# Prompt attention in a hybrid decoder layer: values as weights on column halves, probabilities scaled one step ahead of their turn, output feature-major

## The reference, cut to what matters

```python
s = jnp.einsum('bnqkgd,bnskd->bnkgqs', qb, kband, preferred_element_type=jnp.float32) * (HEAD_DIM ** -0.5)
p = _sink_softmax(s, sinks, mask[None, :, None, None])      # exp(s - m) / (sum + exp(sink - m))
o = jnp.einsum('bnkgqs,bnskd->bnqkgd', p.astype(v.dtype), vband)
...
h = h + (ga * (oa @ w_oa) + gb * (ob @ w_ob)) @ w_out
```

## Time and profile before

| | |
|---|---|
| median of 3 runs | 3545.36 us (3543.18 to 3545.62) |
| the profiled execution, its own time | 3547.21 us |
| span of the profiled execution, first to last instruction | 3545.4 us |
| busy: PE, DVE, ACT, POOL | 97%, 49%, 35%, 7% of the span |
| granted PE clock, mean | 0.977 |
| granted PE clock in the delta stage: first group (210 to 555 us), second group (1216 to 1384 us) | 0.86, 1.00 |

### The profile page before, as it was taken

How to read it: one execution, slowest core, us unless ns; L and a number is a source line. 1 busy time by engine, 2 the same in 40 slices (tenths; PEclk the granted TensorE clock), 3 DMA queues, 4 the chain that set the end, 5 groups by cost and what they waited for, 6 DMA issues and landing times.

```text
span 3545.4 us, 52950 instructions
## 1 busy us (share of the span) xinstructions
PE 3430.2 (97%) x21860; PEld 2912.6 (82%) x21860; DVE 1730.3 (49%) x3115; ACT 1257.6 (35%) x2414; POOL 253.2 (7%) x289
## 2 busy tenths in 40 slices
PE   6979999999999999999999999999999999999998
PEld 6868779999999777888878877888887877788886
DVE  3844334543446744554345744554344755454343
ACT  3323324322223544432224544432223544432222
POOL 1211000000002101000001201000000311000000
PEclk9868989999999999999999999999999999999999
DMA  4101012322233211333233211233234211233232
GB/s 171 60 20 50 31 32 71 104 90 85 87 133 105 68 43 43 107 101 95 94 132 121 74 43 43 84 114 98 92 93 165 78 44 42 73 114 99 96 95 81
DMA packets 88558, 298.66 MB, mean 84 GB/s; under 512 B 12272, under 2 KB 14272, under 8 KB 87664
## 3 DMA queue, kind: packets, MB, share of 16 engines
q1 hardware_dynamic: 88320, 295.28, 25.8%
HBM read 283.63 MB, written 12.62 MB: 84 GB/s over the span
## 4 chain that ended last, share of the span: by engine, by line
PE 51%; issue 11%; ACT 2%; DMA 1%; DVE 1%; SPq 0%; POOLq 0%; POOL 0%; DVEq 0%
PE bank L734 42%; PE bank L922 1%; PE bank L1159 1%; DMA raw<-in_wstream 1%; PE bank L1150 1%; PE bank L1162 1%; PE bank L897 1%; PE bank L1093 1%; PE bank L909 1%; PE bank L1067 1%; PE bank L1073 0%; PE bank L950 0%; ACT junk L1510 0%; PE bank L995 0%; PE bank L1104 0%
## 5 line engine op out<-in xcount | busy, mean ns | idle before, releaser
L734 PE MATMUL bank<-hnT,wh 128*128 128x512 f32 (+1 forms) x3520 | 931.4, 352 | 0.0
L1675 DVE TENSOR_TENSOR wl<-raw,wh 128x1024 fp32r<-128x1024 f32 x480 | 595.0, 1240 | 662.5 <-ACT wh L1316 661.1
L734 PE MATMUL bank<-xnT,wh 128*128 128x512 f32 (+2 forms) x2560 | 742.1, 376 | 13.9 <-DVE d_dT L1927 11.1
L734 PEld LDWEIGHTS bank<-hnT,wh 128*128 128x128 f32 x3520 | 619.4, 188 | 91.4 <-issue 0.2
L1316 ACT CAST wh<-raw 128x1024 fp32r<-128x1024 f32 x480 | 500.4, 1043 | 392.7 <-PE bank L734 337.8
L734 PE MATMUL bank<-hnT,wl 128*128 128x512 f32 (+1 forms) x1760 | 622.2, 354 | 0.0
L734 PEld LDWEIGHTS bank<-xnT,wh 128*128 128x128 f32 x2560 | 450.7, 194 | 86.7 <-DVE d_dT L1927 12.4
L734 PE MATMUL bank<-hid,wh 128*128 128x512 f32 (+1 forms) x1760 | 468.2, 354 | 5.2 <-DVE wl L1675 4.0
L734 PE MATMUL bank<-xnT,wl 128*128 128x512 f32 (+2 forms) x1280 | 469.3, 367 | 0.0
L734 PEld LDWEIGHTS bank<-hnT,wl 128*128 128x128 f32 x1760 | 330.6, 188 | 45.8
L734 PEld LDWEIGHTS bank<-hid,wh 128*128 128x128 f32 x1760 | 309.5, 188 | 53.2 <-DVE wl L1675 6.0
(11 more groups left out here) (309 smaller groups left out, 3916.5 us busy)
## 6 DMA issues: line engine op xcount, KB each, us to landing
raw<-in_wstream SPq DMA_DIRECT2D x472, 512.0 KB, 3.5
xr<-in_x_prompt SPq DMA_DIRECT2D x16, 512.0 KB, 5.6
xT<-in_xT SPq DMA_DIRECT2D x4, 2048.0 KB, 12.2
hT<-in_xT SPq DMA_DIRECT2D x4, 2048.0 KB, 8.6
out_yp_out<-hT SPq DMA_DIRECT2D x16, 512.0 KB, 2.9
raw<-in_wstream SPq DMA_DIRECT2D x8, 528.0 KB, 3.8
Sb<-in_state_delta SPq DMA_DIRECT2D x1, 2048.0 KB, 10.3
out_ds_out<-Sb SPq DMA_DIRECT2D x1, 2048.0 KB, 6.4
```

Source lines behind the costliest of these rows:

```text
L734: ins = nc.tensor.matmul(*a, **k)
L1675: v_.tensor_tensor(wl[n % HL][:, 0:m], raw[:, n % RAW, 0:m], wh[n % HL][:, 0:m].bitcast(F32), ALU.subtract).then_inc(sem("lo_done"), 1)
```

## The change

It has four parts.

1. The value products swap their operands. `vn` (128 keys by 64 features) is the weight, put on the left or the right half of the array's columns, and `pTm` moves, two heads (256 columns) at a time. Four products instead of eight; the result in bank 4 is feature-major, the two key/value heads in the two partition halves.
2. The denominators can't be applied behind such a product, so DVE scales the probabilities in `sc` (128x1024) between exp and transposes, in a step of its own, `scale`; the copy of bank 4 becomes a plain one.
3. To make room for that step the tables are moved: in `IN_DELTA` transposes from 6 and 11 to 7 and 12, the first values from 7 to 8; in `IN_CONV` transposes from 6 and 8 to 7 and 9, values from 7 and 9 to 8 and 10; in `IN_DELTA_S` inputs, scores and exps one step earlier.
4. The 16 transposes of the `z` stage go in each group; ACT and DVE read `qkv` in place of a bank.

```diff
-IN_DELTA = dict(inputs=2, scores=(3, 8), exp=(5, 10), transposes=(6, 11), values=(7, 13))
-IN_DELTA_S = dict(inputs=1, scores=(2, 6), exp=(3, 7), transposes=(4, 8), values=(5, 13))
+IN_DELTA = dict(inputs=2, scores=(3, 8), exp=(5, 10), scale=(6, 11), transposes=(7, 12), values=(8, 13))
+IN_DELTA_S = dict(inputs=0, scores=(1, 5), exp=(2, 6), scale=(3, 7), transposes=(4, 8), values=(5, 13))
-IN_CONV = dict(inputs=4, scores=(5, 7), exp=(5, 7), transposes=(6, 8), values=(7, 9))
+IN_CONV = dict(inputs=4, scores=(5, 7), exp=(5, 7), scale=(6, 8), transposes=(7, 9), values=(8, 10))
...
             def att_transposes(t, gk):
                 r = round_of(t, gk)
-                pe.wait_ge(*made("pexp_done", r + 1))
+                pe.wait_ge(*made("att_p", 2 * t + gk + 1))
...
                 claim(4, "oa_done", r + 1)
-                for y in range(GQ):
-                    ps = slice(HD * (y % NKV), HD * (y % NKV + 1))
-                    for s in range(2):
-                        last = nc.tensor.matmul(bank[4][:, HD * y:HD * (y + 1)], pTm[:, 2 * y + s, :], vn[:, s, ps],
+                turned = pTm[:].rearrange("p (x y) n -> p x y n", x=2)
+                for s in range(2):
+                    for half in range(NKV):
+                        ps = slice(HD * half, HD * (half + 1))
+                        last = nc.tensor.matmul(bank[4][ps, 0:2 * P], vn[:, s, ps], turned[:, :, 2 * half + s, :],
                                                 start=s == 0, stop=s == 1)
...
                 feature_block("z", j, (1, 0)[j % 2], 2, "z_ps", "z_silu", j + 1)
-                b = (6, 7)[j % 2]
-                claim(b, "oT_lo", (j + 1) * (1 + F))
-                for t in range(NT):
-                    last = nc.tensor.transpose(bank[b][:, P * t:P * (t + 1)], qkv[:, t + 1, P * j:P * (j + 1)], c("ident"))
-                last.then_inc(sem("oaT_ps"), 1)
...
-                act.wait_ge(*made("oaT_ps", j + 1))
-                act.copy(oT[0][:, j, MAIN], bank[(6, 7)[j % 2]][:]).then_inc(sem("oT_hi"), 1)
+                if j == 0:
+                    act.wait_ge(*made("oa_done", round_of(NT - 1, NKV - 1) + 1))
+                act.copy(oT[0][:, j, MAIN].rearrange("p (t n) -> p t n", t=NT), qkv[:, 1:, P * j:P * (j + 1)]).then_inc(sem("oT_hi"), 1)
...
                     r = round_of(t, gk)
+                    if k == where["scale"][gk]:
+                        denominators(r, GQ)
+                        settle()
+                        v_.tensor_tensor(sc[:], sc[:], bc(st[:, 20:20 + GQ], [P, GQ, 2 * P]), ALU.mult).then_inc(sem("att_p"), 1)
                     if k == where["transposes"][gk]:
-                        denominators(r, GQ)
                         dve.wait_ge(*made("pT_ps", r + 1))
...
                         dve.wait_ge(*made("pv_ps", r + 1))
-                        v_.tensor_tensor(qkv[:, t + 1, 256 * gk:256 * (gk + 1)].rearrange("p (a e) -> p a e", a=GQ),
-                                         bank[4][:, 0:GQ * HD].rearrange("p (a e) -> p a e", a=GQ),
-                                         bc(st[:, 20:20 + GQ], [P, GQ, HD]), ALU.mult).then_inc(sem("oa_done"), 1)
+                        v_.tensor_copy(qkv[:, t + 1, 2 * P * gk:2 * P * (gk + 1)], bank[4][:, 0:2 * P]).then_inc(sem("oa_done"), 1)
...
-                v_.tensor_tensor(oT[1][:, j, MAIN], bank[(6, 7)[j % 2]][:], oT[0][:, j, MAIN].bitcast(F32), ALU.subtract).then_inc(sem("oT_lo"), 1)
+                v_.tensor_tensor(oT[1][:, j, MAIN].rearrange("p (t n) -> p t n", t=NT), qkv[:, 1:, P * j:P * (j + 1)],
+                                 oT[0][:, j, MAIN].bitcast(F32).rearrange("p (t n) -> p t n", t=NT), ALU.subtract).then_inc(sem("oT_lo"), 1)
```

More of the change, by code:

```diff
@@ L101 @@
         (0, 4, 4):
-            "oaT_ps ob_hi ob_lo prod_done z_silu",
+            "ob_hi ob_lo prod_done z_silu",
         (0, 5, 4):
@@ L110 @@
         (0, 8, 8):
-            "hn_hi hn_lo hsq_done mix_f mix_hi mix_lo pT_rd0 sqc_done sum_ps ysq_done",
+            "att_p hn_hi hn_lo hsq_done mix_f mix_hi mix_lo pT_rd0 sqc_done sum_ps ysq_done",
         (0, 9, 0):
@@ L395, in program @@
         A_done QK_done X_done Y_ps Y_done m_done PT_ps PT_done X_ps X_rd DT_ps XY_done WU_ps WT_rd U_rd WS_ps u_done ob_rd
-        QB_zero small_p o_ps dS_ps S_done osq_done orr_done ob_done gate_ps gate_e gate_done z_ps z_silu obT_ps ob_lo oaT_ps
+        QB_zero small_p att_p o_ps dS_ps S_done osq_done orr_done ob_done gate_ps gate_e gate_done z_ps z_silu obT_ps ob_lo
         oT_hi oT_lo prod_done mix_ps mixS_ps mix_rd mix_f mix_hi mix_lo state_out act_g dve_g gate_eS act_pre
```

## The result

The changed kernel takes 3576.43 us (median of 4 runs, 3574.91 to 3577.99), the kernel before beside it 3545.49 us (4 runs, 3543.18 to 3546.72): ratio 1.0089, interval 1.0077 to 1.0101. It is 31 us slower, where +12.5 us was forecast and the range ended at 3572. The profiled execution's span is 3575.2 us against 3545.4, so the two traces differ by 29.8 us.

A forecast was written before the change was run, and what follows sets the result against it. PE, busy 97% of the span, was taken to bound the kernel by its work plus waits. Terms -5.2 + 6 - 1 + 1 + 8.7 + 3 = +12.5 us on 3547.2 gave about 3557.5 us as median, range 3545 to 3572.

The forecast's parts named there:

- Value products: PE's value step in each of 32 rounds: 1.82 us falls to 1.17, gaining 0.65 a round if PE isn't waiting.
- z blocks: Removed transposes save PE 0.43 us in each of blocks 0 to 2, nothing in block 3; 5.2 us over four groups.
- Scaling on DVE: DVE's added step takes about 1.2 us; probabilities are ready 1.6 us after DVE turns to them.
- Delta tiles: Nine tiles of groups 2 to 4: new PE waits outweigh cheaper values, +0.65 us a tile, +6 us, bounds -1 to +13.
- Rival B: Waits are covered because DVE reaches the sum earlier against PE; delta tiles -8 us, total about 3541 us; chance 0.08.
- Beside tile S: Cheaper values against attention inputs now ahead of the Gram product and added scaling: +1 us, between -3 and +3.
- Conv stages: Groups 2 to 4: second round's scores wait 3.3 us for just-filled banks; +2.9 us a stage, +8.7, between +6 and +11.
- the end of the stage keeps its distances, so nothing is given back: Conv stages: after the second round's transposes find their probabilities ready, the stage's end keeps its distances; nothing is given back.
- The clock: More PE waits and holes may bring clock dips, one earlier dip being worth 1.9 us: +3 us, 0 to +10.
- rival A: Column halves don't overlap, so a value step takes 1.9 us and 21 us aren't saved: 3578 us; chance 0.06.
- PE busy less by 20 us or more: Sign that the prediction is right: PE's busy time falls by 20 us or more at a longer span.

The follow-up runs named there:

- none: Changed kernel with the step tables of before and no scaling of the probabilities in the prompt's attention; 3515.02 us.
- scale_first: Changed kernel with DVE's scaling moved ahead of the weight split of the same step, at steps 6 and 11; 3560.48 us.
- the filled kernel: Changed kernel with idle products that nobody reads at three places where PE waits, in groups 2 to 4; 3562.41 us.
- before_filled: Kernel before the change with 9 idle products ahead of its 2.2 us wait at line 951 in groups 2 to 4; 3542.35 us.
- mend_later: `early_bank7` plus scaling ahead of the split, inputs beside tile S as before; in later groups values at step 9, quarter of 12 at 11; 3531.0 us.
- bank7: Changed kernel with the values of tile 0 beside the conv blocks put in bank 7 instead of bank 4; 3562.51 us.
- early_bank7: `bank7` with the first attention round beside the conv blocks started one block earlier; 3549.79 us.

## Why the prediction was wrong, point by point

- **Value products: right.** Forecast 1.17 us, bounds 0.96 to 1.9; measured 1.02. The allowance of 0.1 for a change of shape wasn't needed. The rule of "TensorEngine Tiling (Array Packing)", section "Theoretical Speedup", in the Trainium skill, up to twice as fast, taken in full, would have given the lower bound of 0.96 (an estimate, from the earlier trace rows); the step lies between that and the row of the scores (1.07).
- **z blocks: right.** 1.3 us a group forecast, 1.14 to 1.29 measured.
- **Scaling on DVE: right** in size (1.2 us forecast, 1225 ns mean of 32). What stands ahead of it was not: with the sum at 0.70 us the probabilities are ready 2.2 us after DVE turns to them (1250.02 to 1252.19) and not 1.6 in eight of the nine delta tiles, and in the ninth it turns to them 0.6 us late. In each case it is POOL's product, now beside the weight split, that overlaps it.
- **Delta tiles: mechanism right, size off.** The three waits were forecast at 0.9, 0.4 and 0.6 us and are 1.14 (1.52 in the ninth tile), 0.44 and 0.55. The tile costs +1.05 us instead of +0.65. Against the -1.5 of `none` that is 2.55, of which the idle times are 2.13. The other 0.4 is mostly the way of counting: an idle begins at the end of a record, a step is counted from start to start, and so counted the three come to 1.53, 0.51 and 0.62 (from line 1068, 1074 or 1094 to the product that waited, less the same step before). The bounds of -1 and +13 took in two of the three waits, not all. `scale_first` shows that the first wait carries 1.35 of it: nine tiles, 12 us. Rival B had this mechanism, DVE's lead over the split that waits for ACT's rounding, at -8 us; it just isn't what the changed kernel does.
- **Beside tile S:** +1 forecast within -3 to +3, +2.6 measured. The wait of the Gram product for ACT's copy was put at 2.4 us and is 3.25.
- **Conv stages: the step that failed.** The wait ahead of the scores was found and sized (3.3 forecast, 3.01 measured). What failed is the sentence that "the end of the stage keeps its distances, so nothing is given back". Moving the second values from step 9 to 10 moves DVE's copy of them behind the taps of block 10, and bank 4 is claimed again by line 968 just then. I followed the moved banks 1 and 2 to their next user and not bank 4. That is 2.2 us of PE in each of three stages, 6.6 us: the term is 15.6 us instead of 8.7, outside its own bound of 11.
- **The clock: mechanism right, number of falls wrong.** +3 us forecast, 0 to +10; the filled kernel puts it at 3.7 to 4.1 us a conv stage, 11.5 us in all. I had one dip of the earlier trace rows as a sample, behind the one hole that was there. The conv stages now have six falls, two in each, at the two new waits, and one of the two lasts into the next block. That is 1.9 us a fall, the price that I had put on one; this was partly luck, since the dip of the earlier trace rows itself was worth 0.8 (`before_filled`). Three of the six stand behind the wait that the conv term had missed.

The trace came out 17.3 us above the sum. The conv term is short by 15.6 - 8.7 = 6.9 of it and the clock by 11.5 - 3 = 8.5; all other terms together by 1.9. The sum named the right side and the right chief place, and the range missed since both terms came out above their own upper bounds, the clock partly because the conv term had: the one hangs on the other. That 3576 is close to rival A's 3578 is chance; A wanted value steps of 1.9 us. Of what the text said would show it, "PE busy less by 20 us or more" was wrong too: slow products count as busy, so the clock's falls hide much of the saving (10.7 us less; 31.9 less in `none`, whose page has PE at 3398.3).

## What to carry to other kernels

When a step table is moved, list for every buffer of every moved step who claims it next, and whose queue its release now stands in; the wait that was missed here was on a bank whose own step had only moved by one. Put the added operation of a shared engine ahead of that engine's waits, not behind them. Count a hole of some 2 us in a busy PE at more than its length: here the clock behind it cost up to as much again, and work in the hole, even useless work, gave that back.

## What the runs showed of the hardware that was not expected

- Eight records of 256 columns on alternating column halves take 1.02 us, as little as eight on alternating row halves (1.07), and 24 us of PE time over 32 rounds come back whole when nothing is waited for (`none`).
- The lower clock comes behind holes of 2.2 us, but not always. The wait of 2.2 us at line 951 is followed by it in two of the three later groups before, in two after, in all three of `mend_later` and in none of `bank7`. It also came behind shorter ones: behind the 1.5 us ahead of line 909's conv transposes in one group of `early_bank7` and in two of `mend_later`, and in two delta tiles of `early_bank7` behind waits of 1.1 and 0.4 us. What decides that is open.
- In the first group two moved pieces of PE's order changed the clock from 0.90 to 0.84 over 140 us, with PE equally busy (65.3 and 65.2 of 70 us against 65.9 twice).
- A DVE and a POOL operation that overlap can hold each other up. In each of the nine delta tiles POOL's product of 128x256 now overlaps DVE's weight split of 128x1024 by 0.7 to 0.9 us, and either it takes 1.48 us instead of 0.74 and DVE's next sum 0.70 instead of 0.15, or the split takes 1.81 us instead of 1.23. This is read from the times of the rows; no run moved POOL's product alone.
